# A hybrid decoder step: four heads of the second row tile between the last row products, two heads to a bank pair, value buffers in input columns, values gathered ahead of keys

## The chip, the cores and the metric

The kernel runs on one core of a Trainium2 chip. Its time is the device time of one execution in microseconds (us). The engines are TensorE (PE), VectorE (DVE), ScalarE (ACT), GpSimd (POOL) and SyncE (SP), which work side by side and wait for each other by semaphores. POOL issues all gathers of this kernel, each a DMA whose source rows are given by a list of indices.

## The reference

One trunk layer for 528 prompt rows (16 learned ones ahead of 512) and for 32 decode tokens (8 sequences of 4). The rows are normed and multiplied by one wide input matrix; a convolution branch and an attention branch are gated, merged, projected and added; a gated feed-forward part with a short convolution follows. The attention keeps, for each query, the best keys by an indexer's score:

```python
idx = indexer_topk(qi, wi, ki_all, qpos, n_keep)          # 132 of the prompt's keys, 256 of 4100 cached ones
logits = einsum('bqhd,bqkhd->bqhk', q, k_sel) * ATTN_SCALE + bias     # 8 heads of 64
p = softmax(where(rel >= 0, logits, -inf))
o = einsum('bqhk,bqkhd->bqhd', p, v_sel)
y_b = o.reshape(b, t, 512) @ w_b_out
x = x + (sigmoid(ga) * y_a + sigmoid(gb) * y_b) @ w_o
```

For a decode token, `k_sel` and `v_sel` are 256 rows of 512 floats from a paged cache.

## The kernel before

The 560 rows (32 decode, 528 prompt) lie in five row tiles of 128, the last of 48. `xnT` holds the normed input with channels on partitions, 560 columns in each of eight blocks.

**Prompt attention** is dense with a mask (`selb`, large negative numbers where a key isn't kept). Heads are numbered on: head `a` is head `a % 8` of row tile `a // 8`. Tile 0 is done by functions of its own (`first_...`), and heads 8 to 39 in a loop on each engine. A head passes: `logits_pair` (PE, for two heads at once: q times k and the mask into bank pair `G`), `at_max` (DVE: scales, adds the bias, keeps the row's extreme, writes `pr`), `at_exp` (ACT), `turn_probs` (PE: transposes into `UB`), `probs_in` (ACT: copies to `pT`), `weighted_sum` (PE: times the values, into `TB`). When a tile's eight heads are done, `at_out` (DVE) divides and `turn_out` (PE) and `take_out` (ACT) transpose it into `oT`.

**Row products** `("q", r)` and `("k", r)` (`natural` on PE, eight matmuls with 512 columns each) give q and k of row tile r. ACT copies them out of the banks (`pair_in`), squares them (`pair_squares`), DVE norms them (`pair_factor`, `pair_scale`), PE transposes them (`pair_trans`), ACT takes them (`take_pair`) and stores k (`pair_out`). Tile 4's `pair_trans(4)`, `pair_out(4)` and `take_pair(4)` come inside the loop of heads, at head `AT_LAST_ROW`.

**Turns of banks.** The list `products` gives every user of the two bank pairs `G[0]` and `G[1]` a number; even numbers have one pair, odd ones the other. `begin` waits until the user two places back has freed its pair, `ready` waits until a product is complete.

**Decode attention** works per token i (32 of them, in two groups of 16). POOL gathers 256 key rows (`keys(i)`, two DMAs into `ksel[i % 3]`) and 256 value rows (`values(i)`, two DMAs into one of nine value buffers). `keys(i)` waits for key product i - 3, `values(i)` from 9 on waits for the matmuls of value i - 9 (`pv_used`). Value 6 also waits for the last `pair_trans` and for the stores of k, since buffers 6 to 8 lie on the row tiles' own buffers. `key_product(i)` (DVE, a product of two SBUF operands and a sum) makes the logits. Per group, `hot_buckets` (DVE), `tokens` and `bias` (PE) make the bias, then follow `group_logits`, `group_max`, `group_prob`, `group_probs`, four times `values_quad` (PE, four tokens of 16 matmuls in all, weights in `psT`), and `group_out` (DVE writes `ovm`, PE multiplies, DVE copies into `oT`).

**Order.** Each engine runs its list in the order of the code. Tables say at which head the loop takes up which piece of the decode work, one lookup per head:

```python
AT_MAX, AT_WEIGHTS, AT_PROBS, AT_OUT = {14: 0, 30: 1}, {15: 0, 31: 1}, {16: 0, 32: 1}, {28: 0, 39: 1}
AT_QUADS = {17: 0, 19: 1, 22: 2, 27: 3, 33: 4, 35: 5, 37: 6, 39: 7}
```

After the loop PE goes on with the products `("yb", n)` (`transposed`, `w_b_out` times `oT`), which need all of `oT`, and from there on with the output projection and the feed-forward part. In the rows, the matmuls of `natural` are L743, `pair_trans` L755, `first_turn` L1118, `logits_pair` L1069 and L1074, `turn_probs` L1089, `weighted_sum` L1100, `turn_out` L1135, `tokens` L1149, `values_quad` L1187 and L1196, PE's part of `group_out` L1204, `yb` L763. On DVE `at_max` is L1720, `key_product` L1749 and L1751. Every gather is L2464 on POOL.

## Time and profile before

| | |
|---|---|
| median of 3 runs | 1231.4 us (1226.59 to 1232.13) |
| the profiled execution | 1233.26 us, its span 1231.5 us |
| PE busy | 1122.3 us (91%) |
| DVE busy | 781.3 us (63%) |
| ACT busy | 310.2 us (25%) |
| POOL busy | 181.3 us (15%) |
| granted TensorE clock, mean | 0.948 |

Busy time is what the hardware profiler counted per engine in one execution. DMA-issuing instructions don't count as busy on the other engines; on POOL, gathers are counted. Times in the rows are microseconds from the span's start. The heads 8 to 39 lie between about 534 and 699 us.

### The profile page before, as it was taken

The page shows a single profiled execution, that of the slowest core. Times are in us where ns is not written, and L with a number is a line of the kernel's source. Part 1 is how long each engine was busy: PE and PEld are TensorE (multiplying, and loading weights), DVE is VectorE, ACT ScalarE, POOL GpSimd, SP SyncE. Part 2 cuts the span into 40 slices and gives each one's busy share as a digit, 9 for nine tenths or more (in the row PEclk, how much of TensorE's full clock was granted, in tenths as well). Part 3 has the DMA queues.
Part 4 walks back from the last instruction along what each step waited for, and adds up shares of the span by engine and source line. Part 5 has one row for each costly group of instructions (what it writes and reads, how often), then busy time and mean ns, then how long its engine had stood idle before and what let it go on. Part 6 is the DMA issues. An engine that isn't in the chain of part 4 may idle for free. (4 is left out here: it accounts for less than half of the span.)

```text
span 1231.5 us, 16971 instructions
## 1 busy us (share of the span) xinstructions
PE 1122.3 (91%) x6816; PEld 904.7 (73%) x6816; DVE 781.3 (63%) x1567; ACT 310.2 (25%) x633; POOL 181.3 (15%) x191
## 2 busy tenths in 40 slices
PE   5999799999789999978759799999999999989995
PEld 3668688664567733445435489999999999989995
DVE  5299999688799899877642163286666656622220
ACT  2111233222201234423213214223232212322120
POOL 0011110000011223155673200000000000001102
PEclk9999899999899999976878899999999999999998
DMA  9110550013243545255785522032323232223320
GB/s 306 45 68 7 179 182 1 18 51 137 69 169 122 162 156 174 75 162 157 226 269 176 158 90 60 1 93 79 99 74 103 70 103 69 72 76 91 113 80 28
DMA packets 109160, 134.51 MB, mean 109 GB/s; under 512 B 8085, under 2 KB 76077, under 8 KB 108036
## 3 DMA queue, kind: packets, MB, share of 16 engines
q1 hardware_dynamic: 90661, 76.52, 20.6%
q0 software_dynamic: 13344, 45.70, 11.9%
q10 hardware_dynamic: 5077, 11.20, 2.6%
q8 instruction: 54, 0.88, 0.3%
q14 instruction: 24, 0.20, 0.1%
HBM read 127.89 MB, written 5.51 MB: 108 GB/s over the span
## 5 line engine op out<-in xcount | busy, mean ns | idle before, releaser
L1253 PE MATMUL G<-xnH,whi 128*128 128x274 f32 x704 | 205.3, 292 | 1.4 <-DVE aext L1895 1.0
L1254 PE MATMUL G<-xnL,whi 128*128 128x274 f32 x704 | 203.5, 289 | 0.0
L1255 PE MATMUL G<-xnH,wlo 128*128 128x274 f32 x704 | 202.9, 288 | 0.0
L978 PE MATMUL G<-xnT,wring 128*128 128x280 f32 x512 | 137.8, 423 | 8.8 <-ACT sgb L1973 3.7
L1835 DVE TENSOR_TENSOR wlo<-wraw,whi 128x2048 fp32r<-128x2048 f32 (+1 forms) x38 | 76.4, 2011 | 92.2 <-ACT whi L2337 91.4
L1253 PEld LDWEIGHTS G<-xnH,whi 128*128 128x128 f32 x704 | 132.4, 188 | 1.8 <-issue 1.2
L1254 PEld LDWEIGHTS G<-xnL,whi 128*128 128x128 f32 x704 | 133.4, 189 | 0.1
L1255 PEld LDWEIGHTS G<-xnH,wlo 128*128 128x128 f32 x704 | 133.1, 189 | 0.0
L978 PEld LDWEIGHTS G<-xnT,wring 128*128 128x128 f32 x512 | 98.7, 199 | 38.3 <-issue 6.4
L2464 POOL DMA_INDIRECT ksel<-in_cache_k_dram,gather_row x64 | 72.7, 1136 | 336.7 <-DVE gather_row L1701 180.1
L1253 PE MATMUL G<-hfH,whi 128*128 128x274 f32 x352 | 103.2, 293 | 0.0
L1254 PE MATMUL G<-hfL,whi 128*128 128x274 f32 x352 | 102.6, 291 | 0.0
L1255 PE MATMUL G<-hfH,wlo 128*128 128x274 f32 x352 | 102.6, 291 | 0.0
L1439 DVE SCALAR_TENSOR_TENSOR hT<-gluT,cols,hT 128x528 f32<-128x528 f32 x120 | 99.8, 832 | 4.2
L2337 ACT ACTIVATE whi<-wraw 128x2048 fp32r<-128x2048 f32 (+1 forms) x38 | 63.9, 1681 | 72.8 <-DMA wraw<-in_w_down_dram 72.8
L1253 PEld LDWEIGHTS G<-hfH,whi 128*128 128x128 f32 x352 | 67.3, 191 | 0.1
L1254 PEld LDWEIGHTS G<-hfL,whi 128*128 128x128 f32 x352 | 67.2, 191 | 0.0
L1255 PEld LDWEIGHTS G<-hfH,wlo 128*128 128x128 f32 x352 | 67.1, 191 | 0.0
L763 PE MATMUL G<-xnT,wring 128*128 128x280 f32 x256 | 61.9, 400 | 0.0
L2506 POOL DMA_DIRECT2D out_p_ffn_conv_dram<-tailn x1 | 0.6, 559 | 407.1 <-ACT tailn L2409 407.1
L2464 POOL DMA_INDIRECT vsel<-in_cache_v_dram,gather_row x54 | 53.9, 998 | 34.4 <-PE UB L1196 18.5
L743 PE MATMUL G<-wring,xnT 128*128 128x512 f32 (+1 forms) x128 | 56.6, 596 | 2.3 <-ACT nats L2131 1.2
(408 smaller groups left out, 1999.5 us busy)
## 6 DMA issues: line engine op xcount, KB each, us to landing
wraw<-in_w_up_dram SPq DMA_DIRECT2D x44, 512.0 KB, 5.1
wring<-in_w_in_dram SPq DMA_DIRECT2D x8, 2048.0 KB, 7.8
wraw<-in_w_down_dram SPq DMA_DIRECT2D x16, 704.0 KB, 4.7
qB<-scr_q SPq DMA_DIRECT2D x32, 256.0 KB, 3.6
wring<-in_w_in_dram ACTq DMA_DIRECT2D x3, 2048.0 KB, 9.8
wring<-in_w_o_dram SPq DMA_DIRECT2D x2, 2048.0 KB, 8.2
toep<-scr_toep SPq DMA_DIRECT2D x1, 2432.0 KB, 15.7
wqi<-in_w_in_dram SPq DMA_DIRECT2D x2, 1024.0 KB, 9.5
```

The lines of the kernel that those rows point to most:

```text
L743: last = pe.matmul(out[0:rows, 0, 0:n], xnT[:, k, t0:t0 + rows], w[:, k, :], start=(k == 0), stop=(k == KM - 1))
L763: last = pe.matmul(out[:, i, 0:b - a], w[:, j, c:c + P], x[:, j, a:b], start=(j == 0), stop=(j == k - 1))
L978: last = pe.matmul(out[:, i, 0:b - a], w[:, j, c:c + P], x[:, j, a:b], start=(j == 0), stop=(j == depth - 1))
L1253: pe.matmul(out, w_hi, x_hi, start=start, stop=False)
L1254: pe.matmul(out, w_hi, x_lo, start=False, stop=False)
L1255: return pe.matmul(out, w_lo, x_hi, start=False, stop=stop)
L1439: dve.scalar_tensor_tensor(out, a, w[:, k:k + 1], out, ALU.mult, ALU.add).then_inc(S["dve_tap"], 1)
L1835: step(dve.tensor_tensor(fview(wlo, i), fview(wraw, i), fview(whi, i).bitcast(F32), ALU.subtract), S["w_split"])
L2337: step(act.activation(fview(whi, i), fview(wraw, i), ACT.Copy), S["w_high"], free=True)
L2464: pool.indirect_dma_start(dst[:, c, :], None, cache, bass.IndirectOffsetOnAxis(ap=gather_row[:, i // 4, (i % 4) * 2 + c:(i % 4) * 2 + c + ...
L2506: pool.dma_start(OUT["p_ffn_conv"][0, 0], tailn[0:FEXT, :]).then_inc(s_out, 16)
```

## The change

Heads 8 to 11 are taken out of the loop and placed by hand among the products of row tile 4: `natural` gets a function that it calls half way through its eight matmuls. `LOOP_FROM` is 12. Heads below 32 (`LAST_TILE`) see fewer than 512 keys, so two of them fit one bank each: they share one bank pair and one number in `products`, the even head's `at_max` signals `at_even`, the odd one's frees the pair. Value buffers 0 to 2 and `psT` lie in columns 0 to 511 of `xnT`, which `("k", 3)` reads last, `psnew` lies elsewhere. POOL issues values 0 to 2 ahead of key 17, values 3 to 5 ahead of key 19, values 6 to 8 ahead of key 20, and keys 20 to 27 ahead of value 9. All tables move on.

```diff
-    vsel = [q(f"vsel{i}", [P, 2, 512]) for i in range(3)]
-    psT = q("psT", [P, 2, 16, 4 * N_HEADS])
-    psnew = q("psnew", [NS, P])
+    vsel = [xnT[:, 2 * i:2 * i + 2, 0:512] for i in range(3)]
+    psT_bank = xnT[:, 6:8, 0:512]
+    psT = psT_bank.rearrange("p c (i h) -> p c i h", h=4 * N_HEADS)
+    psnew = nc.alloc_sbuf_tensor_at("psnew", [NS, P], F32, offset=IDX + 10240)
...
-    products += [("q", 1), ("q", 2), ("k", 1), ("k", 2), ("lg", 0), ("q", 3), ("k", 3), ("tp", 0), ("q", 4), ("k", 4)]
-    TOKENS_AT = {11: 0, 13: 1}
-    for a in range(N_HEADS, ATTEND):
-        products.append(("at", a))
+    products += [("q", 1), ("q", 2), ("k", 1), ("k", 2), ("lg", 0), ("q", 3), ("k", 3), ("tp", 0), ("at", 8), ("q", 4), ("at", 10), ("k", 4), ("at", 12)]
+    TOKENS_AT, LAST_TILE, LOOP_FROM = {15: 0, 17: 1}, ATTEND - N_HEADS, 12
+    for a in range(LOOP_FROM + 2, ATTEND):
+        if a % 2 == 0 or a >= LAST_TILE:
+            products.append(("at", a))
...
-    AT_MAX, AT_WEIGHTS, AT_PROBS, AT_OUT = {14: 0, 30: 1}, {15: 0, 31: 1}, {16: 0, 32: 1}, {28: 0, 39: 1}
-    AT_QUADS = {17: 0, 19: 1, 22: 2, 27: 3, 33: 4, 35: 5, 37: 6, 39: 7}
+    AT_MAX, AT_WEIGHTS, AT_PROBS, AT_OUT = {19: 0, 31: 1}, {20: 0, 32: 1}, {21: 0, 33: 1}, {29: 0, 39: 1}
+    AT_QUADS = {22: (0,), 23: (1,), 25: (2,), 28: (3,), 34: (4,), 36: (5,), 38: (6,), 39: (7,)}
-    AT_KEYS = {11: 16, 13: 17, 14: 18, 15: 19, 16: 20, 17: 21, 18: 22, **{a: a + 3 for a in range(20, 29)}}
-    AT_LAST_ROW, AT_LAST_MASK = 11, 19
+    AT_KEYS = {a: a + 4 for a in range(12, 28)}
+    AT_LAST_ROW, AT_LAST_MASK = 15, 22
...
-        natural(("q", 4), 512)
         pair_trans(2)
-        first_sums()
-        natural(("k", 4), 512)
+        logits_pair(8)
+
+        def beside_query():
+            first_sums()
+            turn_probs(8)
+
+        natural(("q", 4), 512, beside_query)
+        weighted_sum(8)
+        turn_out(0)
+        turn_probs(9)
+        logits_pair(10)
+
+        def beside_key():
+            weighted_sum(9)
+            turn_probs(10)
+
+        natural(("k", 4), 512, beside_key)
+        weighted_sum(10)
+        turn_probs(11)
         pair_trans(3)
-        logits_pair(N_HEADS)
-        for a in range(N_HEADS, ATTEND):
+        logits_pair(12)
+        weighted_sum(11)
+        for a in range(LOOP_FROM, ATTEND):
...
         def values(i):
             if i == 0:
+                ready(pool, ("k", NT - 2))
+            if i == 3:
                 ready(pool, ("k", NT - 1))
...
+        for i in range(3):
+            values(i)
         for i in range(17, 19):
             keys(i)
-        ready(pool, ("k", NT - 1))
-        for i in range(6):
+        for i in range(3, 6):
             values(i)
-        for i in range(19, 21):
+        keys(19)
+        for i in range(6, 9):
+            values(i)
+        for i in range(20, 28):
             keys(i)
-        for i in range(21, NS):
-            values(i - 15)
+        for i in range(28, NS):
+            values(i - 19)
             keys(i)
-        for i in range(NS - 15, NS):
+        for i in range(NS - 19, NS):
             values(i)
```

DVE takes heads 8 to 13 by hand as well: `at_max(8)`, `at_max(9)`, `pair_factor(3)`, `at_out(0)`, `pair_scale(3)`, `at_max(10)`, `prompt_mask(3)`, `at_max(11)`, `key_product(15)`, `at_max(12)`, `pair_factor(4)`, `at_max(13)`, `pair_scale(4)`. ACT has `at_exp`, `probs_in` and `take_out(0)` of these heads between the copies of tile 4's products. Key product 20 stands behind the scan of head 17 in both kernels.

On PE, from the last 128-row product to the loop, before (L743 the products, L755 `pair_trans`, L1127 `first_sums`, L1069 and L1074 the logits, L1089 `turn_probs`):

```order
L743 MATMUL G<-wring_70,xnT 128x512 x8
L1118 MATMUL G<-pack,pr_109 128x96 x8
L743 MATMUL G<-wring_71,xnT 48x512 x8
L755 MATMUL TB<-pack,nats_141 128x128 x4
L755 MATMUL UB<-pack,nats_141 128x128 x4
L1127 MATMUL TB<-vnat,pT8a 96x64 x6
L1127 MATMUL TB<-vnat,pT8b 96x64 x2
L743 MATMUL G<-wring_70,xnT 48x512 x8
L755 MATMUL TB<-pack,nats_140 128x128 x4
L755 MATMUL UB<-pack,nats_140 128x128 x4
L1069 MATMUL G<-kT,qT 128x224 x2
L1074 MATMUL G<-selb,identb 128x224 x2
```

The same place in the changed kernel, from the first half of `("q", 4)` to the second half of `("k", 4)` (L745 the products, L1134 `first_sums`, L1096 `turn_probs`, L1107 `weighted_sum`, L1142 `turn_out`):

```order
L745 MATMUL G<-wring_71,xnT 48x512 x4
L1134 MATMUL TB<-vnat,pT8a 96x64 x6
L1134 MATMUL TB<-vnat,pT8b 96x64 x2
L1096 MATMUL UB<-pack,pr_110 128x128 x2
L745 MATMUL G<-wring_71,xnT 48x512 x4
L1107 MATMUL TB<-vnat,pT 128x64 x2
L1142 MATMUL UB<-pack,onat 128x96 x4
L1096 MATMUL UB<-pack,pr_111 128x128 x2
L1075 MATMUL G<-kT,qT 128x224 x2
L1080 MATMUL G<-selb,identb 128x224 x2
L745 MATMUL G<-wring_70,xnT 48x512 x4
L1107 MATMUL TB<-vnat,pT 128x64 x2
```

Turns, sums and logits of heads 8 to 11 now stand inside and between the two products of row tile 4, where before the products stood alone and the first logits came behind them.

On POOL, behind the last stores of v, before (`ksel` are key gathers, 105, 77 and 78 its three buffers; `vsel` value gathers, values 0 to 5, then 6 to 8):

```order
L612 DMA out_p_v_dram<-vnat 48x512
L2464 DMA ksel_105<-in_cache_k_dram,gather_row 128x512 x2
L2464 DMA ksel_77<-in_cache_k_dram,gather_row 128x512 x2
L2464 DMA vsel_152<-in_cache_v_dram,gather_row 128x512 x2
...
L2464 DMA vsel_159<-in_cache_v_dram,gather_row 128x512 x2
L2464 DMA ksel_78<-in_cache_k_dram,gather_row 128x512 x2
L2464 DMA ksel_105<-in_cache_k_dram,gather_row 128x512 x2
L2464 DMA vsel_160<-in_cache_v_dram,gather_row 128x512 x2
L2464 DMA ksel_77<-in_cache_k_dram,gather_row 128x512 x2
L2464 DMA vsel_161<-in_cache_v_dram,gather_row 128x512 x2
```

The same place in the changed kernel (a gather into `xnT` is one of values 0 to 2; `vsel_156` to `vsel_158` are values 6 to 8, the `ksel_105` behind them is key 20):

```order
L2509 DMA xnT<-in_cache_v_dram,gather_row 128x512 x6
L2509 DMA ksel_105<-in_cache_k_dram,gather_row 128x512 x2
L2509 DMA ksel_77<-in_cache_k_dram,gather_row 128x512 x2
L2509 DMA vsel_153<-in_cache_v_dram,gather_row 128x512 x2
L2509 DMA vsel_154<-in_cache_v_dram,gather_row 128x512 x2
L2509 DMA vsel_155<-in_cache_v_dram,gather_row 128x512 x2
L2509 DMA ksel_78<-in_cache_k_dram,gather_row 128x512 x2
L2509 DMA vsel_156<-in_cache_v_dram,gather_row 128x512 x2
L2509 DMA vsel_157<-in_cache_v_dram,gather_row 128x512 x2
L2509 DMA vsel_158<-in_cache_v_dram,gather_row 128x512 x2
L2509 DMA ksel_105<-in_cache_k_dram,gather_row 128x512 x2
```

Three values have moved ahead of keys 17 and 18, and values 6 to 8 all stand ahead of key 20, where before key 20 came ahead of value 6.

## Rows read from the trace of the kernel before

**Rows 1.** Windows: busy us (instructions) per engine, granted clock, DMA share, GB/s

```profile
534.00:570.00 36.00, 27.76 (x109) 18.39 (x109) 22.88 (x49) 10.63 (x33) 17.76 (x18) 0.62 0.53 155
...
605.00:645.00 40.00, 23.26 (x133) 13.46 (x131) 20.75 (x29) 8.49 (x19) 31.48 (x29) 0.80 0.79 264
```

**Rows 2.** Timeline of PE, 640 to 700: start, us, instruction, [idle before, releaser]

```profile
644.41 1.89 PE L1204 MATMUL TB<-pack,ovm 128*128 128x16 f32 x8 [7.20 <-DVE ovm L1780]
...
668.89 1.92 PE L1196 MATMUL UB<-vsel,psT 128*32 128x512 f32 x16
...
691.03 1.07 PE L1196 MATMUL UB<-vsel,psT 128*32 128x512 f32 x2 [3.72 <-DMA ksel<-in_cache_v_dram,gather_row]
...
698.85 31.88 PE L763 MATMUL G<-qT,wring 128*128 128x280 f32 x128 [0.47 <-issue]
```

**Rows 3.** Timeline of POOL: value 6, key 31, value 25, last issue

```profile
569.80 0.95 POOL L2464 DMA_INDIRECT vsel<-in_cache_v_dram,gather_row  x1 [0.31 <-issue]
...
632.02 1.61 POOL L2464 DMA_INDIRECT ksel<-in_cache_k_dram,gather_row  x1 [0.30 <-issue]
...
671.07 0.94 POOL L2464 DMA_INDIRECT vsel<-in_cache_v_dram,gather_row  x1 [15.28 <-PE UB L1196]
...
687.32 0.95 POOL L2464 DMA_INDIRECT ksel<-in_cache_v_dram,gather_row  x1 [0.30 <-issue]
```

**Rows 4.** Timeline of DVE: the first pass of the last key product

```profile
641.28 1.22 DVE L1749 TENSOR_TENSOR ksel<-ksel,qB 128x1024 f32<-128x1024 f32 x1 [6.64 <-DMA ksel<-in_cache_k_dram,gather_row]
```

**Rows 5.** Timeline of PE, 516 to 561: products of tile 4, first heads

```profile
516.51 7.07 PE L743 MATMUL G<-wring,xnT 128*48 128x512 f32 x16
...
533.89 0.65 PE L1069 MATMUL G<-kT,qT 64*128 64x224 f32 x4
...
537.60 0.44 PE L1089 MATMUL UB<-pack,pr 128*128 128x128 f32 x2 [2.77 <-ACT pr L2228]
...
543.68 1.11 PE L1100 MATMUL TB<-vnat,pT 128*128 128x64 f32 x4
...
559.92 0.62 PE L755 MATMUL UB<-pack,nats 48*128 48x48 f32 x4
```

**Rows 6.** ACT's store of tile 4's keys; DMA issues with KB, us to landing

```profile
557.99 0.34 ACTq L612 DMA_DIRECT2D out_p_k_dram<-nats  x1
...
vsel<-in_cache_v_dram,gather_row POOLq DMA_INDIRECT x54, 3.8
...
ksel<-in_cache_k_dram,gather_row POOLq DMA_INDIRECT x35, 4.1
...
out_p_k_dram<-nats ACTq DMA_DIRECT2D x1, 96.0 KB, 3.1
```

**Rows 7.** Timeline of DVE: a head's scan in row tile 2

```profile
578.97 0.51 DVE L1720 CUSTOM_DVE_ANT_0 pr<-G,toep 128x352 f32<-128x352 f32 x1
```

**Rows 8.** Timeline of PE, heads 18 to 28 and the group's pieces

```profile
580.04 0.64 PE L1179 MATMUL TB<-pack,lts 128*128 128x128 f32 x2
...
589.37 0.55 PE L1089 MATMUL UB<-pack,pr 128*128 128x128 f32 x3
...
604.89 1.38 PE L1100 MATMUL TB<-vnat,pT 128*128 128x64 f32 x6
...
606.69 1.92 PE L1196 MATMUL UB<-vsel,psT 128*32 128x512 f32 x16 [0.42 <-DMA vsel<-in_cache_v_dram,gather_row]
...
630.00 3.60 PE L1196 MATMUL UB<-vsel,psT 128*32 128x512 f32 x16 [0.50 <-DMA vsel<-in_cache_v_dram,gather_row]
...
636.21 1.00 PE L1100 MATMUL TB<-vnat,pT 128*128 128x64 f32 x8
...
667.84 1.12 PE L1187 MATMUL UB<-vnat,psnew 32*128 32x512 f32 x2
```

**Rows 9.** Timelines of DVE and POOL: a key product and a gather's issue

```profile
567.46 1.22 DVE L1749 TENSOR_TENSOR ksel<-ksel,qB 128x1024 f32<-128x1024 f32 x1
...
567.69 1.80 POOL L2464 DMA_INDIRECT ksel<-in_cache_k_dram,gather_row  x1 [0.30 <-issue]
```

More of the change, by code:

```diff
@@ L1060, in logits_pair @@
             t0, rows, seen, _ = att_tile(r)
-            outs = [begin(("at", a + odd)) for odd in range(2)]
+            if a < LAST_TILE:
+                both = begin(("at", a))
+                outs = [both[:, odd, :].unsqueeze(1) for odd in range(2)]
+            else:
+                outs = [begin(("at", a + odd)) for odd in range(2)]
             if h == 0:
@@ L1075, in logits_pair @@
                                      start=False, stop=True, skip_group_check=True)
-                last.then_inc(g_ready, 1)
+                if odd or a >= LAST_TILE:
+                    last.then_inc(g_ready, 1)
         def turn_probs(a):
@@ L2314, in _ @@
         step(last, S["newhot_loaded"], free=True)
-        act.wait_ge(S["at_clear"], 2)
-        at_exp(N_HEADS)
-        for a in range(N_HEADS, ATTEND):
+        at_exp(LOOP_FROM)
+        for a in range(LOOP_FROM, ATTEND):
             r, h = a // N_HEADS, a % N_HEADS
```

64 lines of the change are left out of this document (43 added, 21 removed).

## The prediction

> **What bounds the kernel now.** I read the windows of the trace first, then the timelines of TensorE (PE), GpSimd (POOL), VectorE (DVE) and ScalarE (ACT) from the last row products to the output projection. The whole change lies in that stretch. Everything behind the first `yb` product at 698.85 [rows 2] stays as it is, so what counts is when that product starts. The reader is to see in [rows 1] that no engine fills the stretch: between 605 and 645 PE is busy for 23 of 40 us and POOL for 31, and between 534 and 570 TensorE's granted clock is 0.62, so for much of it the engine ran at 1.2 GHz.
>
> The chain runs backwards like this. `yb` follows the last value quad, which waits 3.72 us for a gather (PE at 691.03) [rows 2]. That gather is POOL's last issue, at 687.32. Values 25 to 31 can only be issued once the first quad of group 1 (quad 4) has freed their buffers: POOL sat for 15.28 us before 671.07, and quad 4 ended at 668.89 + 1.92 = 670.8 [rows 2, 3]. From quad 4's end to `yb` there are 28.0 us, fourteen issues, one landing and the last quad: a fixed tail. Quad 4 in turn needs all 32 key products. DVE waited 6.64 us at 641.28 for the last gathered key [rows 4], and PE, which wanted DVE's `ovm` behind it, stood still for 7.20 us [rows 2]. That key was issued at 632.02 because POOL alternates keys and values, one token (two issues) of each [rows 3]. So POOL's queue sets the pace up to 644, PE and DVE up to 671, POOL again to the end.
>
> **The change, part by part.** *Moved buffers.* Values 0 to 2 land in input columns and need only product `("k", 3)`. Their six issues (1.25 us each, 7.5) move under the last two products instead of standing behind them. The psT memset keeps its size (128x1024) and costs what it did. Shared banks: the same matmuls and scans, one semaphore instead of another: 0. With one turn for two heads the next logits wait for the odd head's scan of the pair before, which is what they waited for before too: also 0. If that cover is gone, the price is one scan, 0.5 us per pair.
>
> *Heads 8 to 11 between the products.* From 516.5, where `("q", 4)` starts before [rows 5], PE now has, ahead of head 12's logits: both products (7.07 each), two pair turns (1.1 each), two logits pairs (0.95), first sums (1.65), four turns of probabilities (0.44), three weighted sums (0.55, half of the 1.11 that the row shows at the lower clock) and an output turn (0.6): 23.9 us. Two waits are new: turn 9 stands behind the exponent, which on ACT stands behind the copy of `("q", 4)` (0.6 us), and turn 11 behind copy, squares and exponent after `("k", 4)` (2.1 us). Head 12's logits start at 543.1, where before head 8's started at 533.89 [rows 5]. So four heads are done for 9.2 us.
>
> *What is late next.* Value 6 needs the last row tile's turn and the store of its keys, both at head 15 now. Before, from head 8's logits to that store's issue there were 24.1 us and to the turn's end 26.6 [rows 5, 6]; the block of four heads with the two token products is the same, only its heads are 12 to 15. So the store is issued at 567.2 and lands 3.4 us later, at 570.6. Value 6 was issued at 569.80 [rows 3]: no gain is left there, although the heads are ahead. And the new order puts values 6 to 8 ahead of key 20. Six issues of 1.25 us (0.94 plus 0.30 between) end at 578.1, key 20's second issue starts at 579.3 and lands at 583.4 (4.1 us) [rows 6]. DVE is free for its product from about 571 and waits 12 us. Queued behind that product on DVE is head 18's scan, and PE waits for it: product 2.4 (two passes of 1.22), scan 0.45 [rows 4, 7], exponent 0.8, so head 18 turns at 587.1. Before, it turned at 589.37 [rows 8], but with quad 0, the group's logits and its probabilities behind it. These are still to come now.
>
> *Heads 18 to 22.* Before they took 589.37 to 606.3, 16.9 us with quad 1 in it (1.92). Now, without that quad but with the group's logits (about 1.4), probabilities (1.1 with their wait), the new tokens' product (1.12 at the upper clock) and quad 0 (1.92) [rows 8]: 20.6 us, to 607.7. Before, quad 0 ended at 589.4.
>
> *Values 9 to 15.* Value 9 waits for quad 0. From 607.3 to value 15's second issue are 21 issues, since keys 28 to 31 stand between: 26.3 us, plus what DVE adds to them, plus 3.8 to land [rows 6]. DVE does add. The issue at 567.69 took 1.80 us where one takes 0.94, and DVE's product of two SBUF operands ran from 567.46 to 568.68 [rows 9]: the issue began its 0.94 us only when the product was over. Five key products fall into this stretch; I take 3.0 us (ends: 0, and 5 x 0.86 = 4.3). The Trainium skill, SBUF — State Buffer, in its part on which operations take the shared pair, has a product of two SBUF inputs contend with GpSimd's reads only and infers that descriptor writing goes on. By that the 3.0 would be 0; the row says otherwise. With the row, value 15 lands at 640.4. PE reaches quad 3 after heads 23 to 28 and quads 1 and 2, which took 636.21 + 1.00 - 606.69 - 3.60 = 26.9 us before [rows 8]: at 634.6. It waits 5.8 us.
>
> *To the end.* Quad 3 takes 3.6 at the lower clock, head 29 takes 3.8 and the `ovm` products 1.9: 649.7, where before they ended at 646.3 [rows 2]. From there to quad 4's end were 24.5 us. Head 29 (3.8) leaves that span and head 34 with its logits (3.3) enters: 24.0, so 673.7. That is 2.9 us later than 670.8. The tail of 28.0 is unchanged: its fourteen issues are still behind quad 4. PE has one head fewer in it and waits longer for the same gather.
>
> **Sum:** +2.9 us. The profiled execution took 1233.26 (span 1231.5 and 1.8 around it), which gives 1236.2. It lies 1.9 above the median of the runs, 1231.4, so against that median I forecast 1234. Bounds: the DVE price from 0 to 4.3; the half-clock part of quad 3 from 0 to 1.7.
>
> **Rivals.** *A, the sum above, 1234:* the lead of four heads is given back at key 20 and at value 15. Against it: both waits rest on landing times, and 2 us either way in each stay unseen.
>
> *B, faster, about 1225.* Heads 12 to 15 run at the full clock, since PE comes to them from dense products. Then DVE's queue sets that block (factor and scale of the last pair, three key products, one `hot_buckets`, 19 us from 544): the store lands at 567.4, 3.2 us earlier, and so does all behind. With no DVE price on the issues (3.0), quad 3 at the full clock (1.7) and a shorter head 29 and `ovm` (1.5), the sum is 2.9 - 9.4 = -6.5. For it speaks that the 7.20 us stall goes away in any case, since the last key is issued about 5 us earlier. If both new waits vanish (5.5 and 5.8) it is -8.4, the lower end.
>
> *C, slower, about 1241.* The wait of 5.5 us before head 18 drops TensorE to 1.2 GHz for all of heads 18 to 22. The trace shows the like: after the wait of 2.77 us before 537.6 [rows 5], a weighted sum takes 1.11 instead of 0.55. Twenty us of which some 14 are matmul time at a mixed clock become 27, quad 0 ends at 614, and value 15 and the tail follow: +6.5 on the sum, 1240.7. It decides if the granted clock over the five heads is nearer 0.5 than 0.75. The Trainium skill, TensorE: Matmul & The Clock Gate, on the gate oscillating, tells the same of loops that wait in each round; by it C would be the rule here and not the exception. Heads 18 to 22 before took 16.9 us [rows 8], which is the upper clock for most of them, behind short waits only, so I give it less.
>
> That the change does nothing is part of A: the tail hides anything that doesn't move quad 4.
>
> **How the numbers follow.** A 0.40, B 0.33, C 0.27. A measurement here tells about 0.5% (6.2 us) from no change. A lies within it, B just beyond it on one side, C on the other: faster 0.33, same 0.40, slower 0.27. Since B and C hold more than half together, the range covers both, 1222 to 1243; A's own range is 1229 to 1239.
>
> **What the trace after would show.** Values 0 to 2 issued near 516; `("k", 4)` ending near 539 instead of 533; POOL idle until about 570 before value 6; a DVE wait of about 12 us before key 20's product and a PE wait of 5 before head 18; quad 0's end near 608; a PE wait of 3 to 8 us for a value gather before quad 3; no wait for the last key; quad 4's end near 674 and 28 us from there to `yb`. The forecast is wrong if value 6 starts before 566, if quad 0 ends before 603 or after 612, or if the tail is not 28 us long.

## The result, and the profile after

| | before | after |
|---|---|---|
| median | 1230.2 us (4 runs, 1226.59 to 1232.13) | 1248.17 us (4 runs, 1246.72 to 1251.49) |
| profiled execution | 1233.26, span 1231.5 | 1246.84, span 1245.0 |
| granted clock, mean | 0.948 | 0.934 |
| ratio, 95% interval | | 1.0153, 1.0119 to 1.0188 |

The change makes the kernel 1.5% slower, 18 us by the medians and 13.6 by the profiled executions. The forecast was 1234, with a range of 1222 to 1243. Ratios and intervals here and below leave out runs more than 1.5% above the fastest of the same kernel in its set, which are one of the kernel shifted by three (1279.6 us), one of quad 4 at head 32 (1259.8) and two of before in set 3 (1266.1 and 1270.7).

Timeline of PE of the changed kernel: start, us, instruction, [idle before, releaser]. L1096 is `turn_probs`, L1203 `values_quad`, L1211 the ovm products.

```profile
585.90 0.90 PE L1096 MATMUL UB<-pack,pr 128*128 128x128 f32 x3 [4.02 <-ACT pr L2264]
...
626.27 1.03 PE L1203 MATMUL UB<-vsel,xnT 128*32 128x512 f32 x1 [5.88 <-DMA xnT<-in_cache_v_dram,gather_row]
...
643.45 3.64 PE L1203 MATMUL UB<-vsel,xnT 128*32 128x512 f32 x16 [5.51 <-DMA vsel<-in_cache_v_dram,gather_row]
...
649.31 1.02 PE L1211 MATMUL TB<-pack,ovm 128*128 128x16 f32 x8
...
684.15 0.83 PE L1203 MATMUL UB<-xnT 128*32 128x512 f32 x2
...
705.33 1.07 PE L1203 MATMUL UB<-xnT 128*32 128x512 f32 x2 [4.83 <-DMA ksel<-in_cache_v_dram,gather_row]
...
713.22 3.14 PE L765 MATMUL G<-qT,wring 128*128 128x280 f32 x6 [0.47 <-issue]
```

POOL and DVE of the changed kernel: value 0, value 6, value 9, value 25, and the product of key 20.

```profile
516.62 1.00 POOL L2509 DMA_INDIRECT xnT<-in_cache_v_dram,gather_row  x1 [19.62 <-PE G L745]
...
569.92 0.94 POOL L2509 DMA_INDIRECT vsel<-in_cache_v_dram,gather_row  x1 [12.33 <-issue]
...
610.03 0.94 POOL L2509 DMA_INDIRECT xnT<-in_cache_v_dram,gather_row  x1 [7.29 <-PE UB L1203]
...
685.25 0.94 POOL L2509 DMA_INDIRECT vsel<-in_cache_v_dram,gather_row  x1 [22.10 <-PE UB L1203]
...
582.21 1.23 DVE L1775 TENSOR_TENSOR ksel<-ksel,qB 128x1024 f32<-128x1024 f32 x1 [10.56 <-DMA ksel<-in_cache_k_dram,gather_row]
```

Windows of the changed kernel (the clock is the third number from the end), and behind them two windows of before.

```profile
585.90:609.80 23.90, 22.30 (x92) 13.36 (x93) 21.66 (x36) 7.08 (x23) 10.99 (x10) 0.58 0.60 189
...
650.30:685.00 34.70, 31.54 (x147) 17.36 (x146) 7.56 (x23) 8.30 (x27) 9.80 (x11) 0.56 0.57 206
685.00:713.20 28.20, 18.45 (x147) 8.91 (x148) 3.92 (x10) 5.30 (x19) 13.23 (x14) 0.80 0.43 131
```

```profile
585.90:606.30 20.40, 16.60 (x96) 8.25 (x95) 15.82 (x23) 5.60 (x15) 13.48 (x14) 0.84 0.69 215
646.30:670.80 24.50, 22.17 (x131) 14.00 (x130) 7.71 (x23) 8.33 (x26) 7.36 (x8) 0.77 0.48 148
```

Read against [rows 2, 3, 5], the places up to 650 us come within 1 us of the forecast, but for quad 0 (609.8 for 607.7) and with one wait, before quad 2, that it didn't have. Values 0 to 2 are issued from 516.62, value 6 at 569.92 (570.6 was forecast), DVE waits 10.56 us for key 20 and PE 4.02 before head 18. Quads 2 and 3 wait 5.88 and 5.51 us for gathers, and the ovm products end at 650.3 (649.7). Then the stretch to quad 4's end takes 34.7 us where 24.0 were forecast. The tail behind it is 28.2 us, as in before. `yb` starts at 713.22 where it started at 698.85: 14.4 us, of which the one stretch holds 10.7 beyond its forecast. From `yb` to the end the two take nearly the same, 532.6 us before and 531.8 after.

### The profile page after: what moved, and what is told of

Read it like the earlier page. It is cut to its first block and busy times, and to the rows that moved or that the text cites. A ratio compares the mean times of both kernels' runs of the same rounds, so it can differ in the third digit from the quotient of the medians.

```text
span 1245.0 us, 16959 instructions
## 1 busy us (share of the span) xinstructions
PE 1137.3 (91%) x6816; PEld 910.3 (73%) x6816; DVE 780.7 (63%) x1567; ACT 310.7 (25%) x633; POOL 179.7 (14%) x191
## 3 DMA queue, kind: packets, MB, share of 16 engines
HBM read 127.89 MB, written 5.51 MB: 107 GB/s over the span
## 5 line engine op out<-in xcount | busy, mean ns | idle before, releaser
L980 PEld LDWEIGHTS G<-xnT,wring 128*128 128x128 f32 x512 | 98.8, 199 | 38.3 <-issue 6.4
L745 PE MATMUL G<-wring,xnT 128*128 128x512 f32 (+1 forms) x128 | 56.9, 596 | 3.2 <-issue 1.8
L765 PEld LDWEIGHTS G<-xnT,wring 128*128 128x128 f32 x256 | 48.2, 190 | 11.6 <-issue 0.5
```

What stands on the lines that cost most here:

```text
L745: last = pe.matmul(out[0:rows, 0, 0:n], xnT[:, k, t0:t0 + rows], w[:, k, :], start=(k == 0), stop=(k == KM - 1))
L765: last = pe.matmul(out[:, i, 0:b - a], w[:, j, c:c + P], x[:, j, a:b], start=(j == 0), stop=(j == k - 1))
L980: last = pe.matmul(out[:, i, 0:b - a], w[:, j, c:c + P], x[:, j, a:b], start=(j == 0), stop=(j == depth - 1))
```

## Experiments

They ran in four sets on four chips, numbered 0, 14, 9 and 2 (sets 1 to 4 of the table). The chip of the two kernels above, whose number is not known, is called the first chip. Before took 1261.9, 1262.8, 1260.3 and 1258.6 us on them (medians), some 30 us more than above, with standstills, in which an engine is idle though the work that it waits for is done (last section). So each kernel is read by its ratio to before in its own set, where 0.001 is 1.26 us. The medians alone give ratios that differ from these by up to 0.002. The changed kernel and before were traced in set 2 alone, and a time that is compared with theirs from another set is a comparison across chips. In this table "stretch" is the time from the end of the ovm products to the end of quad 4 in the profiled execution, with what was inserted.

| kernel | set | ratio to before, 95% | stretch us, clock |
|---|---|---|---|
| changed, again | 2 | 1.0099 (1.0064 to 1.0134) | 32.3, 0.63 |
| before, again | 2 | 1.0001 (0.9969 to 1.0034) | 29.7, 0.78 |
| order of gathers alone | 1 | 1.0075 (1.0045 to 1.0104) | 23.7, 0.80 |
| the same, again | 4 | 1.0105 (1.0072 to 1.0139) | 37.4, 0.73 |
| shared banks alone | 2 | 0.998 (0.9951 to 1.001) | 26.6, 0.76 |
| changed, key 20 first | 1 | 1.0069 (1.0035 to 1.0103) | 27.8, 0.76 |
| changed, quad 4 at head 33 | 1 | 1.001 (0.9985 to 1.0035) | 24.1, 0.79 |
| changed, early quads alone | 4 | 1.004 (1.0013 to 1.0066) | 31.1, 0.67 |
| changed, alternating order | 1 | 1.002 (0.9989 to 1.005) | 26.0, 0.80 |
| changed, waits filled | 2 | 1.0132 (1.0085 to 1.018) | 34.5, 0.55 |
| changed, shifted by three | 3 | 1.0112 (1.0077 to 1.0147) | 24.1, 1.00 |
| changed, shifted by six | 4 | 1.0073 (1.0045 to 1.0101) | 42.6, 0.63 |
| early quads and order | 3 | 0.9949 (0.9927 to 0.9972) | 26.5, 0.74 |
| the same, quad 4 at head 32 | 3 | 0.9933 (0.99 to 0.9965) | 24.7, 0.82 |
| the same, again | 4 | 0.9938 (0.991 to 0.9966) | 28.4, 0.70 |

**Controls: the changed kernel and before, set 2.** No edit in either.

> The changed kernel without an edit, beside the kernel before on the same chip, since the chip of the first four experiments was some 30 us slower with both kernels and its engines stood still in places where no semaphore held them. If the change costs the same there as here, the ratio is 1.011 to 1.019 again. If the loss on the first chip was mostly TensorE's clock and the loss on the second mostly these standstills, the ratio may be anything from 1.005 to 1.02; the waits for key 20 (10 us on VectorE) and for the gathers of quads 2 and 3 must be there on either chip.

> The kernel before without an edit, for its trace on this chip. On the chip of the prediction's trace no engine waited more than 2 us without a releaser between 500 and 760 us. If such standstills are a matter of the chip they are here too, on ScalarE above all, in the stretch in which GpSimd's gathers keep the DMA engines busy; if they are a matter of the changed order they are missing here.

The change costs 1.0099 here, less than the 1.0153 of the first chip; the intervals overlap by little. Both kernels have standstills, so the changed order isn't needed for them. That they are a matter of the chip is not shown: all four later sets have them, and so has before in this set, and the first pair of traces has none over 2 us. The waits for key 20 (10.98 us) and for quad 2 (5.11) are there. The third that was expected, before quad 3, is not: PE stood still for 13.46 and 6.44 us behind quad 2 and came to quad 3 when its values had landed.

**The order of the gathers alone**, in the kernel before:

```diff
-        for i in range(19, 21):
-            keys(i)
-        for i in range(21, NS):
-            values(i - 15)
-            keys(i)
-        for i in range(NS - 15, NS):
-            values(i)
+        keys(19)
+        for i in range(6, 9):
+            values(i)
+        for i in range(20, 28):
+            keys(i)
+        for i in range(28, NS):
+            values(i - 19)
+            keys(i)
+        for i in range(NS - 19, NS):
+            values(i)
```

> The kernel before with one edit: GpSimd issues key 19, values 6 to 8, keys 20 to 27 and only then value 9 and key 28 in turns, which is the order of the changed kernel. Heads, products, banks, buffers and tables stay those of before. Theory W (the order of the gathers makes the loss: late key 20 and late values 9 to 15, and TensorE at the lower clock behind the waits they cause): VectorE waits 8 us or more for key 20 at head 16, TensorE's granted clock falls below 0.7 in the heads behind it, and the kernel is 8 to 18 us slower than before. Theory H (the heads between the products, the shared banks or the tables make the loss, the order is innocent): within 4 us of before. Theory C (the lower clock comes by itself, from where the heads and the pieces stand, whatever waits there are): within 4 us, and the stretch from the ovm products to quad 4 keeps a clock near 0.77.

> The kernel before with the changed order of gathers from key 19 on, once more. On the chip with the standstills it was 9.5 to 11.4 us slower than before, and 16 us of its trace were a standstill of ScalarE while gathers ran. If this job gets a chip without standstills, theory W expects waits of 8 us or more for key 20 and for values, and 8 to 18 us over before; if the loss there was made by the standstills alone, 0 to 4 us. On the same chip again it repeats its result and gives a second trace.

Ratios of 1.0075 and 1.0105: this edit alone makes a loss as large as the whole change's 1.0099. Theory W's total is met, its place is not. DVE does not wait for key 20, whose gather is in time here; PE waits for the values of quads 2 and 3. Timeline of PE of the first of the two executions, and one row of its ACT:

```profile
631.70 3.64 PE L1196 MATMUL UB<-vsel,psT 128*32 128x512 f32 x16 [15.45 <-DMA vsel<-in_cache_v_dram,gather_row]
...
659.18 3.64 PE L1196 MATMUL UB<-vsel,psT 128*32 128x512 f32 x16 [8.45 <-DMA vsel<-in_cache_v_dram,gather_row]
...
681.61 1.97 PE L1100 MATMUL TB<-vnat,pT 128*128 128x64 f32 x8 [16.22 <-issue]
...
680.96 0.60 ACT L2262 ACTIVATE pT<-UB 128x512 f32<-128x512 f32 x1 [30.72 <-remote]
```

(`issue` and `remote` name no engine and no DMA that ended the idle time.) The second execution, and before of set 2, from quad 3 on:

```profile
656.41 3.39 PE L1196 MATMUL UB<-vsel,psT 128*32 128x512 f32 x16 [7.00 <-DMA vsel<-in_cache_v_dram,gather_row]
...
679.65 1.97 PE L1100 MATMUL TB<-vnat,pT 128*128 128x64 f32 x8 [15.22 <-ACT pT L2262]
```

```profile
656.39 3.64 PE L1196 MATMUL UB<-vsel,psT 128*32 128x512 f32 x16
...
670.86 1.97 PE L1100 MATMUL TB<-vnat,pT 128*128 128x64 f32 x8 [6.54 <-issue]
```

Where before waited 0.42 and 0.50 us for values on the first chip [rows 8], 15.45 and 8.45 are waited in the first execution. But these waits are not where the time is lost. Quad 3 ends at 662.8 and 659.8, and at 660.0 in before of set 2, which waits for no value but stands still for 4.98 and 8.53 us on the way. The loss comes behind quad 3: a standstill of 16.22 and 15.22 us where before has 6.54. Quad 4 ends at 708.9 and 701.4 against 693.5. So the loss of this order is shown on chips with standstills alone, mostly as a longer standstill beside a longer run of gathers. Theory H, that the order is innocent, falls for these chips; what the order costs without standstills stays open. The order alone didn't bring the low clock either: the stretch has 0.80, and 0.73 with the 15.22 us of standing still in it, near the 0.77 of theory C, whose time (within 4 us) was missed.

**Shared banks alone**, in the kernel before:

```diff
-        products.append(("at", a))
+        if a % 2 == 0 or a >= LAST_TILE:
+            products.append(("at", a))
```

with the branches of `logits_pair`, `at_max` and `at_exp` that the change has for it.

> The kernel before with one part of the change: heads 8 to 31 go by pairs, both heads of a pair in one bank pair and under one number, the even scan signals for itself and the odd one frees the pair. Order, gathers, tables and buffers stay. The prediction's step (the same matmuls and scans, one semaphore for another: 0): within 3 us of before. Theory B (the next pair's logits now wait for the odd head's scan of the pair before): 12 pairs at 0.5 us, and the lower clock behind them, 4 to 8 us slower.

0.998, 2.5 us under before with an interval that holds 1: no cost, the step priced at 0 holds and theory B falls.

**Key 20 first**, in the changed kernel:

```diff
         keys(19)
+        keys(20)
         for i in range(6, 9):
             values(i)
-        for i in range(20, 28):
+        for i in range(21, 28):
             keys(i)
```

> The changed kernel with one edit: GpSimd issues key 20 ahead of values 6 to 8, not behind them; key 21 and all behind it stay. Theory W: the wait of 10.6 us on VectorE for key 20 goes, and with it the 4.0 us on TensorE before head 18; a wait of some us comes one head later, for key 21. By the time of the wait alone 2 to 4 us faster than the changed kernel (about 1245), and if the low clock of heads 18 to 22 goes with it 5 to 8 us. Theory C: the wait goes and the clock of heads 18 to 22 and of heads 30 to 34 stays at 0.58 and 0.56; within 3 us of the changed kernel.

1.0069 against 1.0099 (another set), 3.8 us by the ratios, with intervals that overlap. The wait goes to key 21, as expected. Timeline of DVE:

```profile
592.50 1.25 DVE L1775 TENSOR_TENSOR ksel<-ksel,qB 128x1024 f32<-128x1024 f32 x1 [8.19 <-DMA ksel<-in_cache_k_dram,gather_row]
```

The clock of the stretch went from 0.63 to 0.76 although this edit lies some 110 us ahead of it. I had not expected that of either theory.

**Quad 4 at head 33**, in the changed kernel: the second group one head earlier.

```diff
-    AT_QUADS = {22: (0,), 23: (1,), 25: (2,), 28: (3,), 34: (4,), 36: (5,), 38: (6,), 39: (7,)}
+    AT_QUADS = {22: (0,), 23: (1,), 25: (2,), 28: (3,), 33: (4,), 35: (5,), 37: (6,), 39: (7,)}
```

and bias to probabilities from 30 to 33 to 29 to 32, the first output from 29 to 28.

> The changed kernel with one edit: the second group's bias, logits, maximum, weights, probabilities and quads 4 to 6 one head earlier, at the heads that they had before (quad 4 behind head 33 and not 34, the first group's output behind head 28). The gathers keep their order. Theory T (the tables make the loss: one head ahead of quad 4 goes straight into the tail): quad 4 ends 3 to 6 us earlier, the time is about 1243 to 1245. Theory W: the same 3 to 4 us for one head and no more; the clock between the ovm products and quad 4 stays below 0.65, since the waits ahead of it stay.

1.001: it takes back 0.9 of 0.99 per cent, 11 us by the ratios, more than either theory gave a head (3 to 6). In the profiled executions quad 4 ends at 703.5 for 712.3. The stretch is 24.1 us at 0.79 where theory W had the clock below 0.65. So the head's own 4 us came with a better clock, and theory W's second half, that the clock hangs on the waits ahead, is in doubt.

**Alternating order**, in the changed kernel: keys 19 and 20, values 6 to 8 in turns with keys 21 to 23, keys 24 to 26, then value 9 and key 27 in turns; quads at 21, 22, 24, 27, 33, 35, 37, 39.

> The changed kernel with before's order of gathers brought back as far as its heads allow: key 20 ahead of value 6, keys 21 to 23 in turns with values 6 to 8, keys 24 to 26, then value 9 and key 27 in turns; quads 0 and 1 one head earlier (21 and 22), quads 2 and 3 at 24 and 27, and the second group at the heads of before. Heads 8 to 11 stay between the products, shared banks and moved buffers stay. Theory W: no wait over 3 us for key 20, quad 2 or quad 3, the granted clock from the ovm products to quad 4 back near 0.75, and 12 to 22 us faster than the changed kernel (1226 to 1236). Theory C: the waits go, but the clock stays below 0.62 there and the time stays above 1240.

1.002, 10 us under the changed kernel by the ratios where 12 to 22 were expected, and no faster than quad 4 at head 33 alone: a miss in time. The waits for key 20 and for quads 2 and 3 are gone and the clock of the stretch is 0.80, as theory W had it and not theory C. PE's quad 0 was still at head 21 and GpSimd stood still for 8.93 us ahead of value 9, and PE stood still for 7.85 and 10.30 us between quads 2 and 3.

**Waits filled.** Is it the standing still that lowers the clock?

```diff
+        def filled(n):
+            for i in range(n):
+                pe.matmul(UB[:, 0, :], ident, vnat[:, 0, :], start=True, stop=True)
...
+            if a == 18:
+                filled(3)
             pe.wait_ge(S["at_exp"], head_at(a) + 1)
...
+            if n in (2, 3):
+                filled(4)
```

> The changed kernel with matmuls that compute nothing used (identity times 512 columns of v, into a bank half that the next turn overwrites) ahead of three of TensorE's waits: three before head 18's turn, four each before the waits for values of quads 2 and 3. Each takes about 0.9 us at the upper clock and 1.8 us at the lower. Nothing of the kernel's own work is left out. Theory W+C (the clock falls because TensorE stands still there, and stays down over the heads that follow): the granted clock over heads 18 to 22 and over the stretch from the ovm products to quad 4 rises above 0.7, and the kernel is 5 to 12 us faster than the changed one although it does 10 to 20 us more work on TensorE. Theory N (the clock of those stretches doesn't hang on these waits): the clock stays near 0.57, and the time is the same or up to 6 us longer.

Windows of this kernel ahead of the end of the ovm products and behind it, and in its timeline the four matmuls ahead of quad 3 with quad 3:

```profile
663.50:675.50 12.00, 11.31 (x69) 6.46 (x69) 2.59 (x6) 2.69 (x8) 6.84 (x8) 1.00 0.62 174
675.50:710.00 34.50, 31.53 (x147) 17.40 (x145) 7.57 (x23) 8.23 (x27) 5.68 (x6) 0.55 0.45 170
```

```profile
666.77 3.65 PE L1087 MATMUL UB<-vnat,pack 128*128 128x512 f32 x8
670.35 1.92 PE L1211 MATMUL UB<-vsel,xnT 128*32 128x512 f32 x16
```

Ahead of quad 3 PE has no wait, and the clock is 1.00 for the 12 us up to the end of the ovm products. (In the control of this set quad 3 had no wait for its values either and also ran in 1.92 us, but the clock of the same 12 us was 0.73.) Behind that the stretch runs at 0.55 all the same, in 34.5 us, and the kernel is not faster (1.0132). Theory W+C falls for the stretch: its clock doesn't hang on those three waits. For heads 18 to 22 this kernel decides nothing, since PE stood still for 5.84 us among them. The Trainium skill, TensorE: Matmul & The Clock Gate, on HAM oscillation (HAM is its name for what gates TensorE's clock), ties the fall in one kernel to a wait for a DMA in each round, and in another to short idle times between groups of matmuls. The trace doesn't agree with the first: the fall comes with PE busy for 31.5 of 34.5 us and no wait over 0.8. No run here tests the second.

**Shifted.** The same unused matmuls behind the ovm products at head 29, three, then six:

```diff
             if a in AT_OUT:
                 group_out(AT_OUT[a])
+            if a == 29:
+                filled(3)
```

> The changed kernel with three matmuls whose result nothing uses behind the ovm products at head 29 (2.6 us at the upper clock, 5.2 at the lower), nothing else. Theory P (the low clock between the ovm products and quad 4 is a matter of when that stretch begins against the rise and fall of the clock, since the same instructions ran there at 0.56, 0.63 and 0.79 in three kernels): shifted by some us, the clock of the stretch changes, most likely up to 0.7 or more, and the stretch from the end of these three to quad 4 takes 25 to 29 us instead of 32 to 35; the time is 3 us shorter to 2 us longer than the changed kernel. Theory Q (the lower clock belongs to this mix of instructions): the clock stays at 0.55 to 0.63 and the time grows by the 5 us.

> The changed kernel with six unused matmuls behind the ovm products at head 29, where the kernel shifted by three had half as many (each 0.86 us at the upper clock, 1.8 at the lower). With three the profiled stretch from the ovm products to quad 4 ran wholly at a granted clock of 1.00 and took 25 us with the three in it, while the unprofiled runs ranged from 1270 to 1280 us at a mean clock of 0.921 to 0.929 and one stood at 1258.5 at 0.936. Theory P (which level the stretch gets depends on when it begins, and differs even between executions): the runs spread by 10 us or more and their times fall with their mean clock; the median is 2 to 6 us over the kernel with three. Theory R (dense matmuls ahead of the stretch lift the clock): the clock of the stretch is above 0.9 again, and most runs lie near the good one, under 1265 on that chip.

Windows of the stretch, shifted by three, then by six, and the second once more from behind the six:

```profile
670.20:694.30 24.10, 21.21 (x153) 12.55 (x152) 7.57 (x23) 7.97 (x27) 5.70 (x6) 1.00 0.56 207
```

```profile
667.90:710.50 42.60, 37.79 (x159) 20.42 (x158) 7.56 (x23) 8.37 (x27) 4.17 (x5) 0.63 0.30 110
...
675.50:710.50 35.00, 30.19 (x147) 17.13 (x144) 7.56 (x23) 8.37 (x27) 0.00 (x0) 0.61 0.17 61
```

The three in the first, with the logits, and the six in the second:

```profile
670.06 2.82 PE L1087 MATMUL UB<-vnat,pack 128*128 128x512 f32 x6
673.25 1.12 PE L1075 MATMUL G<-kT,qT 64*48 64x512 f32 x8
```

```profile
667.80 7.70 PE L1087 MATMUL UB<-vnat,pack 128*128 128x512 f32 x12
```

Without the inserted matmuls one and the same list of instructions took 21.3 us at 1.00 (24.1 - 2.8) and 34.9 at 0.61 (42.6 - 7.7, with one idle time of 2.6). In the changed kernel it took 34.7 at 0.56. The logits (L1075) are 1.12 us in the one and 2.05 in the other. So theory Q, that the lower clock belongs to this mix, falls, and so does theory R, dense matmuls ahead as a cure: six left it low, and no run was under 1265. The good execution is not the kernel's rule either. The profiled one took 1258.5 us at a mean clock of 0.936, four others 1270.7 to 1273.5 at 0.922 to 0.929. Not all of that is the clock of the stretch. Against the control of set 2 (another chip) quad 4 ends 18.0 us earlier, of which 8.2 lie in the stretch and 9.8 ahead of it, where PE stood still less. Theory P stands as far as this: the level of the stretch differs between executions. That the unprofiled ones owe their time to this stretch is not shown, since they have only a mean clock. The expectation of theory P for six missed: the median did not rise over that of three, and the runs spread by 9.3 us and not by 10. What sets the level is not settled.

**Early quads alone**, in the changed kernel:

```diff
-    AT_BIAS, AT_LOGITS = {17: 0, 30: 1}, {18: 0, 30: 1}
-    AT_MAX, AT_WEIGHTS, AT_PROBS, AT_OUT = {19: 0, 31: 1}, {20: 0, 32: 1}, {21: 0, 33: 1}, {29: 0, 39: 1}
-    AT_QUADS = {22: (0,), 23: (1,), 25: (2,), 28: (3,), 34: (4,), 36: (5,), 38: (6,), 39: (7,)}
+    AT_BIAS, AT_LOGITS = {16: 0, 30: 1}, {16: 0, 30: 1}
+    AT_MAX, AT_WEIGHTS, AT_PROBS, AT_OUT = {17: 0, 31: 1}, {18: 0, 32: 1}, {19: 0, 33: 1}, {29: 0, 39: 1}
+    AT_QUADS = {20: (0,), 21: (1,), 25: (2,), 28: (3,), 34: (4,), 36: (5,), 38: (6,), 39: (7,)}
```

> The changed kernel with the first group's pieces early (bias and logits at head 16, quad 0 at 20, quad 1 at 21) and nothing else: gathers in the changed order, quads 2 and 3 at 25 and 28, the second group one head later than before. Theory W (GpSimd stands still until quad 0 frees the buffers of values 0 to 3, so values 9 to 15 are late): value 9 is issued 7 us or more earlier, the wait for the gathers of quads 2 and 3 goes, and the kernel is 3 to 8 us faster than the changed one. The wait for key 20 stays at 10 us. If instead key 20 and the second group's place hold all of the loss: within 2 us of the changed kernel.

Value 9 in this kernel (the changed one of set 2 issues it at 621.24):

```profile
612.04 0.95 POOL L2509 DMA_INDIRECT xnT<-in_cache_v_dram,gather_row  x1 [4.15 <-PE UB L1203]
```

9.2 us earlier, no wait for a gather before quads 2 and 3, and 1.004 against 1.0099, 7 us by the ratios, with intervals that just touch, and 2.5 by the medians. The direction is as theory W had it, in one trace beside one of another chip. PE still stood still for 15.73 us between quads 2 and 3.

**Early quads and order**, in the changed kernel: the first group as just above, quads 2 and 3 at 24 and 27, the second group as with quad 4 at head 33, and on GpSimd

```diff
+        for i in range(19, 23):
+            keys(i)
         for i in range(6, 9):
             values(i)
-        for i in range(20, 28):
+        for i in range(23, 27):
             keys(i)
-        for i in range(28, NS):
-            values(i - 19)
+        for i in range(27, NS):
+            values(i - 18)
             keys(i)
```

> The changed kernel with the first group's pieces as early as its bank allows (bias and logits at head 16, quad 0 at 20, quad 1 at 21, quads 2 and 3 at 24 and 27), the second group's at the heads of before (quad 4 at 33), and GpSimd's order keys 19 to 22, values 6 to 8, keys 23 to 26, then value 9 and key 27 in turns. Theory W (the loss sits in GpSimd's queue, which stands still until quad 0 has freed buffers at head 22): the waits for key 20 and for the values of quads 2 and 3 go, quad 4 ends 15 us or more before that of the changed kernel on the same chip, and the time is 15 to 25 us under the changed kernel, which is under before as well (below 1255 on the slower chip, below 1230 on the first). Rival D (the tail and the clock decide, GpSimd's queue has slack): 9 us under the changed kernel as with quad 4 at head 33 alone, level with before.

> The same as the kernel with early quads, and the second group one head earlier still: the first group's output behind head 27, bias and logits at 28, quad 4 at 32. By the fixed tail of 28 us behind quad 4 a head is worth 3.5 to 4.5 us; a wait of 1 to 2 us for VectorE's ovm behind quad 3 comes on. Theory W: 2 to 4 us under the kernel with early quads. If the last key or value 15 is late for head 27 or 28: nothing gained or 1 to 3 us lost.

> The fastest version so far (early quads, before's alternation of keys and values, quad 4 at head 32), once more, to see whether its gain holds on whichever chip this job gets: ratio to before 0.990 to 0.997 on the chip with standstills. On a chip without them its last waits for gathers should be shorter, and 0.985 to 0.995 is expected; a ratio of 1.00 would say that the gain came only from standstills avoided.

0.9949, 0.9933 and 0.9938: faster than the changed kernel by 1.5% and than before by 0.5 to 0.7%. The last two have quad 4 at head 32 and quad 3's output at head 27. By the intervals the gain of that last head isn't told from nothing. POOL of the kernel with quad 4 at head 33, value 9 and value 25, and PE's quad 0:

```profile
598.64 0.60 PE L1203 MATMUL UB<-xnT 128*32 128x512 f32 x3
...
599.75 1.81 POOL L2509 DMA_INDIRECT xnT<-in_cache_v_dram,gather_row  x1 [0.30 <-issue]
...
684.89 0.95 POOL L2509 DMA_INDIRECT vsel<-in_cache_v_dram,gather_row  x1 [20.18 <-PE UB L1203]
```

GpSimd goes from the keys to value 9 without a pause, and quad 4 frees the tail's buffers at 684.9 where the changed kernel of set 2 does at 712.6, 27.7 us earlier. That overstates the gain: `yb` starts 25.5 us earlier (715.2 for 740.8), the profiled execution of this kernel is one of its fastest and that of the changed one of its slowest, and the gain is 19 us by the ratios, 16 by the medians. In the last kernel's trace GpSimd had a pause of 6.99 us ahead of value 9 again, and its ratio is as good. So the parts of the gain are not told apart: by the ratios early quads alone gave 7 us and quad 4 at head 33 alone 11. The heads between the products are kept in these versions, so they don't stand in the way of a gain. Whether they add to it is not shown: no such order was run without them.

## Why the prediction was wrong

- *Which engine sets the end, and the fixed tail of 28.0 us:* right on this chip, 28.2 measured. In the experiments the tail is not fixed: 28.2 to 29.8 us with quad 4 at head 34, 30.6 to 34.9 at head 33 (before included, 32.7) and 33.6 and 34.3 at head 32. So there a head taken from ahead of quad 4 came back in part behind it.
- *Moved buffers and shared banks at 0:* right for the banks, which alone read 0.998. The buffers were not tested alone.
- *Heads 8 to 11 between the products, and value 6 without a gain:* right to 1 us.
- *Key 20 late:* right in size on the first chip (DVE 10.56 for a forecast 12, PE 4.02 for 5.5). Undone, it gives some 4 us by the ratios, which their intervals don't tell from nothing.
- *Heads 18 to 22:* quad 0's end came at 609.8 for 607.7, 23.9 us after head 18's turn where 20.6 were forecast. Rival C's mechanism was there, a granted clock of 0.58 over these heads, but for 3.3 us at most and not for 6.5, of which a shorter wait before head 18 gave 1.2 back.
- *Values 9 to 15:* the wait before quad 3 was right in size, 5.51 us for 5.8, by luck. The sum took no wait before quad 2, where 5.88 us were waited. From quad 0 to quad 3 PE took 28.2 us with that wait for 26.9 without it, and both PE (637.9 for 634.6) and the last value (643.4 for 640.4) came some 3 us late. Behind quad 3, the turn, the sum and the ovm products then took 3.2 us for 5.7, at a clock of 1.00. So the ovm products ended only 0.6 us after the forecast.
- **The step that failed** is the next: "From there to quad 4's end were 24.5 us. Head 29 (3.8) leaves that span and head 34 with its logits (3.3) enters: 24.0". It measured 34.7. This term is 10.7 of the 14.4 us by which `yb` is late in the profiled execution; 2.9 were forecast. Two things were wrong in it. The larger is the clock. I carried a duration over from before without looking at the clock it contained, 0.77, and after had 0.56. Rival C gave the clock a price, but for heads 18 to 22 alone, so neither the sum nor the range had room for it here. The smaller is the exchange of heads. What enters and leaves, in rows of the changed kernel (third pair of logits, with the turn ahead of it and the sum behind) and of before (a turn and a sum of row tile 3):

```profile
674.61 0.74 PE L1096 MATMUL UB<-pack,pr 48*128 48x48 f32 x5
675.27 2.05 PE L1075 MATMUL G<-kT,qT 64*48 64x512 f32 x8
677.25 1.10 PE L1080 MATMUL G<-selb,identb 128*48 128x512 bf16 x4
678.21 1.45 PE L1107 MATMUL TB<-vnat,pT 128*48 128x64 f32 x10
```

```profile
646.14 1.09 PE L1089 MATMUL UB<-pack,pr 128*128 128x128 f32 x4
647.92 1.97 PE L1100 MATMUL TB<-vnat,pT 128*128 128x64 f32 x8 [0.69 <-ACT pT L2262]
```

The changed kernel has three pairs of logits in the stretch and before has two, at 655.33 and 660.65. So 5.34 us enter and 3.06 leave at the lower clock, +2.3 (at the upper clock +1.4), where the sum had -0.5. By this count the exchange is 2 to 3 of the 10.7 us and the clock some 8. The rows at like clocks agree: 27.8 us at 0.76 with the list of the changed kernel (key 20 first), 24.5 at 0.77 with that of before.

The median is 14.2 us over the forecast, though these terms leave the profiled execution only 10.6 over its 1236.2. The rest is the step from one execution to the medians, and rounding: 1.9 us were taken off because before's profile lay above its median, and the changed kernel's lies 1.3 below.

That the clock can make this stretch long by itself is shown, by the same list of instructions in 21.3 us at 1.00 and in 34.5 to 34.9 at 0.55 to 0.61. That the change brings the lower clock there is shown only as a tendency: in the later sets 0.55 to 0.76 in five traces with quad 4 at head 34 and 1.00 in a sixth, 0.73 to 0.80 in the seven with quad 4 at head 33, as in before on the first chip (0.77), and 0.70 and 0.82 in the two at head 32. It isn't the three waits, since filling them changed nothing. It isn't the order of the gathers alone, which kept 0.80 and 0.73. What it is stays open. What of the change costs time apart from it is shown only on chips with standstills: there the order of the gathers alone makes a loss as large, by the standstill behind quad 3. On the first chip PE, DVE and ACT had no standstill, and the waits for key 20 and for quads 2 and 3 used up the lead of four heads: the ovm products ended 4.0 us later than before, with one head more (3.8) ahead of them. No experiment ran on that chip, so its 18 us are divided by the reading of one trace alone.

## What to carry to other kernels

Where one engine issues all transfers in order, look for the first transfer in its list that waits for a freed buffer, and bring forward the work that frees it before you reorder the transfers; what stands behind it is late by its pause (here quads 0 and 1 two heads earlier gave 7 us by the ratios). A duration that is taken over from the trace of before holds the clock of that execution, so write the granted clock beside it and price every such term at both levels, not only the one behind a new wait. When pieces move to another head, list the instructions that enter and leave the term, since a pair of logits may come in with one head. A lead is only worth what the last fixed part of the chain takes of it: here four heads were ahead at 543 us, for 9.3 us more, and quad 4 was 14.2 us later. And a wait in one trace is not yet a loss: compare the time at which the next piece ends, since another trace may have stood still there for another reason.

## What the runs showed of the hardware

**One program, 1230 us on one chip and 1258.6 to 1262.8 on four others** (medians of the sets). In the profiled executions of before, `yb` starts at 698.9 and at 726.3, and from there to the end both take 532 us. The time is in places where ScalarE and VectorE stand still though the work they wait for is done. ACT of the changed kernel on the first chip, and the same instruction in set 2, with DVE beside it:

```profile
524.38 0.38 ACT L2298 ACTIVATE pT<-UB 128x256 f32<-128x256 f32 x1 [4.01 <-PE UB L1096]
...
524.23 0.20 DVE L1766 RECIPROCAL stat<-stat 96x8 f32<-96x8 f32 x1 [0.73 <-PE TB L1134]
```

```profile
530.12 0.39 PE L1096 MATMUL UB<-pack,pr 128*128 128x128 f32 x2
...
534.35 0.38 ACT L2298 ACTIVATE pT<-UB 128x256 f32<-128x256 f32 x1 [7.81 <-remote]
...
534.35 0.20 DVE L1766 RECIPROCAL stat<-stat 96x8 f32<-96x8 f32 x1 [4.70 <-remote]
```

```profile
523.00:534.30 11.30, 10.85 (x51) 4.59 (x48) 4.67 (x19) 3.45 (x9) 7.43 (x8) 1.00 0.70 202
534.30:540.00 5.70, 3.91 (x18) 1.89 (x19) 4.46 (x8) 2.77 (x8) 0.00 (x0) 0.81 0.04 17
```

On the first chip ACT goes on as the turn ends. In set 2 the turn ends at 530.5, and ACT and DVE both start at 534.35, when the burst of gathers is over (DMA share 0.70 up to there, 0.04 behind). The longest such standstill is that of the order-alone kernel: PE waits for 16.22 and 15.22 us, and ACT starts at 680.96 and 679.0, 1.9 and 3.1 us behind the last gather's issue of a long run. But the end of the burst is not the rule. VectorE went on at 670.48 in the first of these while gathers were issued up to 679.1, and in before of set 2 ACT went on at 670.21 with a DMA share of 1.03 in the 2 us behind it. No row shows what holds the engines. They show that DMAs were in flight: over each idle time of more than 3 us that no engine or DMA ended, between 505 and 745 us in the 15 traces of the later sets, the DMA share was 0.42 or more, in before of set 2 as well. That a longer unbroken run of gathers costs more on such a chip is argued from the order-alone kernel and not tested for itself. Nor is it shown that the chip makes the difference and not something else that the first pair of traces and the later sets don't share.

**The clock** of one stretch of one list of instructions was 1.00 in one kernel and 0.55 in another whose PE was as busy (21.2 of 24.1 us, 31.5 of 34.5). Twelve runs of one kernel (key 20 first) spread from 1260.4 us at a mean clock of 0.932 to 1279.1 at 0.923.
